# Latent attention: standing values, two heads' products alternating, probabilities scaled by GpSimd before they are turned

## The reference

```python
def chunk_causal_attention(q, k, v):            # q, k: 512 x 16 x 96; v: 512 x 16 x 64
...
        sc = jnp.einsum('bqhd,bkhd->bhqk', qi, k, preferred_element_type=jnp.float32) * scale
        mask = key_chunk[None, :] <= q_chunk[:, None]
        p = jax.nn.softmax(jnp.where(mask, sc, -jnp.inf), axis=-1)
        return jnp.einsum('bhqk,bkhd->bqhd', p.astype(v.dtype), v)

def mla_mixer(h, w_dq, q_norm, w_uq, w_dkv, kv_norm, w_ukv, q_gain, k_gain, w_o):
...
    q = (cq @ w_uq).reshape(b, s, MLA_HEADS, MLA_QK)
...
    kv = (ckv @ w_ukv).reshape(b, s, MLA_HEADS, MLA_NOPE + MLA_V)
    k = jnp.concatenate([kv[..., :MLA_NOPE], k_rope], axis=-1)
    v = kv[..., MLA_NOPE:]
    q = rms_norm_2(q, q_gain)
    k = rms_norm_2(k, k_gain)
...
    o = chunk_causal_attention(q, k, v)
    return o.reshape(b, s, MLA_HEADS * MLA_V) @ w_o
```

## Time and profile before

| | us |
|---|---|
| median of 3 runs | 1928.76 (1928.29 to 1929.55) |
| the profiled execution | 1928.52 |
| its span in the profile | 1926.7 |
| TensorE busy over the span | 1912.5 (99%) |
| VectorE | 1215.8 (63%) |
| ScalarE | 940.2 (49%) |
| GpSimd | 49.9 (3%) |
| share of TensorE in the chain that ended last | 96% |
| granted TensorE clock | 0.9 or more in all 40 slices |

### The profile page before, as it was taken

One profiled execution on the slowest core, in us unless ns is written; L12 is line 12 of the kernel. 1 busy time (PEld: TensorE's weight loads), 2 busy tenths in 40 slices (PEclk: granted clock), 3 DMA queues, 4 the chain that ended last, 5 costly groups with the idle time before them and its releaser, 6 DMA issues.

```text
span 1926.7 us, 23396 instructions
## 1 busy us (share of the span) xinstructions
PE 1912.5 (99%) x9546; PEld 1624.5 (84%) x9546; DVE 1215.8 (63%) x1653; ACT 940.2 (49%) x1332; POOL 49.9 (3%) x85
## 2 busy tenths in 40 slices
PE   8999999999999999999999999999999999999999
PEld 6889998888888888898888888888888889888887
DVE  5645553345767676876745868667644357776867
ACT  5333334234645445568754644545565546453543
POOL 1000000000000000010000000000000000000000
PEclk9999999999999999999999999999999999999999
DMA  7233322322341431321013142241232223414141
GB/s 250 76 98 96 92 68 97 110 99 88 108 136 41 153 110 65 103 59 46 23 45 127 49 153 83 92 153 44 89 110 66 88 66 110 142 55 153 36 140 69
DMA packets 163398, 182.47 MB, mean 95 GB/s; under 512 B 7682, under 2 KB 125015, under 8 KB 163163
## 3 DMA queue, kind: packets, MB, share of 16 engines
q1 hardware_dynamic: 160746, 176.67, 28.6%
q0 software_dynamic: 2528, 4.29, 0.8%
q10 hardware_dynamic: 16, 0.00, 0.0%
HBM read 175.62 MB, written 2.11 MB: 92 GB/s over the span
## 4 chain that ended last, share of the span: by engine, by line
PE 96%; DVE 2%; ACT 1%; DMA 0%; issue 0%; SPq 0%; ACTq 0%
PE psum L96 29%; PE psum L98 29%; PE psum L97 29%; PE psum L2274 2%; PE psum L2252 2%; PE psum L2706 1%; PE psum L2262 1%; DVE weights_lo L414 1%; PE psum L578 1%; PE psum L2230 1%; PE psum L2694 0%; PE psum L1025 0%; PE psum L1017 0%; PE psum L996 0%; PE psum L1006 0%; PE psum L994 0%
## 5 line engine op out<-in xcount | busy, mean ns | idle before, releaser
L96 PE MATMUL psum<-norm_T_hi,weights_hi 128*128 128x512 f32 (+1 forms) x1440 | 538.2, 374 | 0.2 <-DVE weights_lo L414 0.2
L98 PE MATMUL psum<-norm_T_hi,weights_lo 128*128 128x512 f32 (+1 forms) x1440 | 533.7, 371 | 0.0
L97 PE MATMUL psum<-norm_T_lo,weights_hi 128*128 128x512 f32 (+1 forms) x1440 | 533.3, 370 | 0.0
L414 DVE TENSOR_TENSOR weights_lo<-raw_weights,weights_hi 128x2048 fp32r<-128x2048 f32 (+3 forms) x136 | 299.1, 2199 | 240.6 <-ACT weights_hi L408 240.4
L408 ACT ACTIVATE weights_hi<-raw_weights 128x2048 fp32r<-128x2048 f32 (+3 forms) x136 | 249.4, 1834 | 189.3 <-PE psum L98 189.3
L98 PEld LDWEIGHTS psum<-norm_T_hi,weights_lo 128*128 128x128 f32 x1440 | 271.2, 188 | 46.8
L96 PEld LDWEIGHTS psum<-norm_T_hi,weights_hi 128*128 128x128 f32 x1440 | 271.3, 188 | 45.9 <-DVE weights_lo L414 0.5
L97 PEld LDWEIGHTS psum<-norm_T_lo,weights_hi 128*128 128x128 f32 x1440 | 271.4, 188 | 45.2
L96 PE MATMUL psum<-weights_hi,act_T_hi 128*128 128x512 f32 (+1 forms) x528 | 204.0, 386 | 0.0
L98 PE MATMUL psum<-weights_hi,act_T_lo 128*128 128x512 f32 (+1 forms) x528 | 203.0, 384 | 0.0
L97 PE MATMUL psum<-weights_lo,act_T_hi 128*128 128x512 f32 (+1 forms) x528 | 202.9, 384 | 0.0
(11 more groups left out here) (317 smaller groups left out, 2458.2 us busy)
## 6 DMA issues: line engine op xcount, KB each, us to landing
raw_weights<-in_ffn_w_dram SPq DMA_DIRECT2D x32, 1024.0 KB, 5.6
scratch<-in_ffn_w_dram SPq DMA_DIRECT2D x32, 1024.0 KB, 5.4
raw_weights<-in_w_in_dram SPq DMA_DIRECT2D x26, 512.0 KB, 5.3
raw_weights<-in_w_in_dram SPq DMA_DIRECT2D x11, 1024.0 KB, 5.3
raw_weights<-in_w_up_dram SPq DMA_DIRECT2D x8, 1024.0 KB, 6.9
scratch<-in_w_up_dram SPq DMA_DIRECT2D x8, 1024.0 KB, 6.8
raw_weights<-in_w_down_dram SPq DMA_DIRECT2D x8, 1024.0 KB, 5.4
scratch<-in_w_down_dram SPq DMA_DIRECT2D x8, 1024.0 KB, 5.2
```

Source lines behind the costliest of these rows:

```text
L96: pe.matmul(out, ah, bh, start=start, stop=False, skip_group_check=more)
L97: pe.matmul(out, ah, bl, start=False, stop=False, skip_group_check=more)
L98: return pe.matmul(out, al, bh, start=False, stop=stop, skip_group_check=more)
L414: dve.tensor_tensor(WL[:, u % 2, 0:c], raw(units[u].slot)[:, 0:c], WH[:, u % 2, 0:c].bitcast(F32), SUB).then_inc(w_lo, 1)
```

## The change

**Products.** `values` now takes a pair of heads. The values of one key tile j stand (128 x 64), and the turned probabilities of all query tiles that need it stream through: 384, 384, 256 and 128 columns, and 128 for the block (0, 0), which has a place of its own. The results come out already turned, head 2p in partitions 0 to 63 and head 2p + 1 in 64 to 127 of bank 6; the instructions of the two heads alternate. The transposes of a pair, the column of ones and the division are gone; `pair_hi` (ScalarE) and `out_lo` (VectorE) read bank 6.

**Scaling.** The exponentials give their running sums (`accum_out`). VectorE inverts them (`factors`: one reciprocal for t = 3 after the first exponential, one for the rest after the last), GpSimd multiplies the probabilities in `SB` by them, four instructions a head, and only then are they turned: `turn` waits for the scaling (`psc`) in place of the exponential (`pex`).

**Places.** `PT` has two buffers of 2048 columns, one per head of a pair; the turned queries and the products of the rotation move to room behind the activations. The products of a pair stand behind the first two projection tiles at heads 1, 3, 5 and 7, and behind the scores, ahead of the transposes, at heads 10, 12 and 14; the last pair is in the tail. The key-value projections of groups 2 and 3 wait for the products that still read the values which they overwrite.

```diff
-                for t in ORDER:
-                    if t == 2:
-                        pe.wait_ge(a1.sem, a1.at(n + 1))
-                    elif t != 0:
-                        pe.wait_ge(pte.sem, pte.at(2 * n + (1 if t == 3 else 2)))
-                    for j in range(t + 1):
-                        mm = pe.matmul(PS[:, 6, t * MV1:t * MV1 + MV1], PT[:, off[t] + j * P:off[t] + j * P + P],
-                                       VN[:, n // 4 % 2, j, n % 4, :], start=j == 0, stop=j == t)
+                def values(pair):
+                    n = 2 * pair + 1
+                    pe.wait_ge(pte.sem, pte.at(2 * n + 2))
+                    pe.wait_ge(a1.sem, a1.at(n + 1))
+                    if pair:
+                        pe.wait_ge(paired.sem, paired.at(pair))
+                        pe.wait_ge(tl.sem, tl.at(pair))
+                    for j in range(NT):
+                        t = max(j, 1)
+                        for b in range(2):
+                            h = n - 1 + b
+                            pe.matmul(PS[b * MV:b * MV + MV, OUT, t * P:S], VN[:, h // 4 % 2, j, h % 4, :], PT[b][:, j, t:NT, :],
+                                      start=j == 0, stop=True, skip_group_check=j > 0)
+                    for b in range(2):
+                        h = n - 1 + b
+                        mm = pe.matmul(PS[b * MV:b * MV + MV, OUT, 0:P], VN[:, h // 4 % 2, 0, h % 4, :], PT[b][:, 3, 2, :],
+                                       start=True, stop=True)
...
                     scores(n + 1)
+                    if n > MH // 2 and n % 2 == 0:
+                        values(n // 2 - 1)
                     turn(n, 0)
...
-                    for what in before:
+                    for what in gemms[:2]:
                         job(what)
-                    values(n)
-                    for what in gemms:
+                    if n < MH // 2 and n % 2:
+                        values(n // 2)
+                    for what in gemms[2:]:
                         job(what)
...
                         act.wait_ge(gemm, gb + 8 * g + 4 + t + 1)
+                        if g > 1:
+                            act.wait_ge(pvd.sem, pvd.at(2 * g - 2))
...
+                for n in range(MH):
+                    for c in range(2):
+                        pool.wait_ge(rcp.sem, rcp.at(2 * n + c + 1))
+                        for t in (ORDER[:1], ORDER[1:])[c]:
+                            z = SB[:, off[t]:off[t] + (t + 1) * P]
+                            pool.tensor_scalar(z, z, rden[:, n % 2, t:t + 1], None, MUL).then_inc(psc.sem, 1)
+                    if n in (4, 8):
...
+                def factors(n):
+                    for c, ts in enumerate((slice(3, 4), slice(0, 3))):
+                        dve.wait_ge(pex.sem, pex.at(4 * n + (1, 4)[c]))
+                        if n > 1:
+                            dve.wait_ge(psc.sem, psc.at(4 * n - 4))
+                        dve.reciprocal(rden[:, n % 2, ts], den[:, n % 2, ts]).then_inc(rcp.sem, 1)
```

126 lines of the change are left out of this document (55 added, 71 removed).

## The result

| | median of the runs, us | lowest to highest | span of the profiled execution | granted clock over the span |
|---|---|---|---|---|
| before | 1928.8 | 1928.3 to 1929.6 | 1926.7 | 1.00 |
| after | 1955.2 | 1947.1 to 1956.3 | 1953.8 | 0.99 |

The ratio is 1.013, its 95% interval 1.0119 to 1.014: the change costs 26 us, 1.3%. The forecast was 1933.2 us with a range to 1949; the time lies above the range. The direction was right and the size was not. The head loop's first scores start at 867.19 us after and at 866.59 before, so nearly all of it comes later than that.

The account below looks back on a forecast made before the run. TensorE, busy 145.1 of 147.0 us at full clock, was taken to bound the stretch. Terms: -18.1 + 9.6 + 8.1 + 2.3 + 1.9 + 1.9 - 1.1 = +4.7 us on 1928.5, so 1933.2 us, range 1929 to 1949.

Parts of the forecast that it names:

- 18.1 us less on TensorE: Head loop: value products and pair transposes of 38.4 us go, new products at 2.54 us a pair cost 20.3.
- the serial rival: TensorE doesn't overlap the two heads' products: 4.42 us a pair, 15.0 us more, 1948 us; chance 0.20.
- 1.2 us behind the key copy, at eight heads: TensorE idle before the next scores at heads 0, 4 and 8 to 13, waiting for ScalarE's key copy: 9.6 us.
- Heads 0, 4, 7 and 12: Stretches from one head's scores to the next: +1.3, -1.4, +1.3 and +1.1 us against before.
- Last head, 1.9 us: Next stage's output product waits for the masks, with 2.6 us of products and pair transposes no longer ahead: 1.9 us.
- Running sums, 4 x 0.1 us: ScalarE's four exponentials of a head each take 0.1 us more for writing a running sum.
- GpSimd's price: GpSimd's scaling costs 0.2 us + 1.2 ns a column: 0.8 us for 512 columns, 1.5 us for the first three.
- The clock: TensorE's clock stays at 1.00; below 1.00 in the stage was a sign of being wrong, making every term larger.
- VectorE beside GpSimd: Two-input VectorE work slows GpSimd; with the table load at head 10 counted 0.6 us, more clashes one or two.
- dear GpSimd: Rival: GpSimd scales at the two-input price, 8 to 10 us more, 1942 us; chance 0.12.
- Cheap: Rival: GpSimd scales at the price of filling, about 3 us less, 1930 us; chance 0.13.
- faster: Rival: the longer way through ScalarE, VectorE and GpSimd is never late, 1923 us; chance 0.07.

Follow-up runs that it names:

- product form: Changed kernel with GpSimd's scaling written as a product of two tensors, the reciprocal repeated along the columns: 1946.5 us.
- product form, filled, small VectorE work: Changed kernel with scaling as two-tensor product, TensorE's gaps filled with identity transposes, VectorE's key normalisation and rotation cut to a sliver: 1935.4 us.
- product form, filled: Changed kernel with GpSimd's scaling as a product of two tensors and TensorE's gaps filled with unread transposes of the identity: 1939.1 us.

## Why the prediction was wrong

The 26.4 us come apart so, each from one pair of kernels, in this order:

| step | from, us | to, us | share |
|---|---|---|---|
| clock at full level (gaps filled) | 1955.2 | 1944.4 | 10.8 |
| GpSimd near the forecast's price (product form) | 1944.4 | 1939.1 | 5.3 |
| VectorE not beside GpSimd | 1939.1 | 1935.4 | 3.7 |
| the rest, over the kernel before | 1935.4 | 1929.0 | 6.4 |

The last line is taken against 1929.0 us, the kernel before as measured beside that run, so the shares sum to 26.2. The forecast's +4.7 us belongs beside the last line. The terms are tied: at the full price the gaps are longer and the clock falls more. In the other order the price comes first with 8.7 us (1955.2 to 1946.5) and the clock second with 7.4 (to 1939.1), so neither can be called the larger; together they are 16.1 us.

**Step by step.** With the three missed terms out, the times from one head's scores to the next can be laid beside the forecast's terms. The table has the change against before of such stretches, from the starts of the scores in the timelines (for instance head 4: 918.90 - 913.57 = 5.33 us after, 913.88 - 907.14 = 6.74 before, -1.41). The forecast is its sum for that head: values and pair transposes gone, products new, its idle terms.

| stretch of head | forecast | product form, filled, small VectorE work | product form, filled | after |
|---|---|---|---|---|
| 0 | +1.3 | +1.2 | +1.2 | +2.9 |
| 1 | +1.3 | +1.8 | +2.6 | +3.3 |
| 3 | +1.3 | +2.1 | +2.1 | +2.1 |
| 4 | -1.4 | -1.4 | -1.4 | -1.4 |
| 5 | +2.2 | +2.0 | +2.7 | +5.6 |
| 7 | +1.3 | +1.2 | +1.2 | +1.2 |
| 9 | +0.8 | +0.8 | +1.6 | +3.8 |
| 10 | +1.7 | +0.7 | +2.0 | +3.6 |
| 11 | +1.1 | +1.2 | +1.5 | +3.8 |
| 12 | +1.1 | +1.1 | +1.1 | +3.9 |

Heads 2, 6 and 8 are left out: -2.6, -2.6 and -1.4 in the forecast and in every kernel. Head 13 has -0.1 in the forecast, and +0.1, +0.1 and +0.7. Over the loop the forecast has 2.9 us, with the old waits of 1.1 us taken off, and the kernel with small VectorE work 4.3. In the profile of that kernel 1.0 us more lies ahead of the first scores (867.63 us for 866.59), where nothing was changed; this start lies between 866.2 and 867.6 us in the profiles.

- *The working*: its terms sum to 4.6 and not 4.7 us. Filling has 0.67 ns a column by its two rows, not 0.69. Its cases give 0.25 for "within" and 0.68 for "slower", for 0.27 and 0.66. Nothing hangs on these.
- *18.1 us less on TensorE*: right, and 1.8 us better. A pair took 2.31 us for the forecast's 2.54, and the serial rival is dead: it takes the other order of instructions to make it true (4.08 us a pair, 12 us). Nor did the change between the whole array and its halves cost much: the first product of a pair starts 889.85 - 889.58 = 0.27 us behind the last projection product, where these follow each other at 0.17.
- *1.2 us behind the key copy, at eight heads*: right in place and number, 1.04 us each, 8.3 in all for 9.6.
- *Heads 0, 4, 7 and 12*: right within 0.2 us. Head 3 was 0.8 low.
- *Last head, 1.9 us*: right within 0.5 us. From the last scores to the end of the last value products before takes 1005.76 + 2.34 - 986.66 = 21.4 us. The product form with fills is 1.7 us longer there, and the forecast 2.2: 2 x 2.54 for the last two pairs, less 2 x 2.18 and 0.44 (the other pair's transposes stood behind this stretch, at 1012.13), and the 1.9. The changed kernel is 3.9 longer, with the clock at 0.95 from 1020 us on.
- *Running sums, 4 x 0.1 us*: right. At 918.74 the four exponentials of head 5 start, and the last sum is out at 921.20 + 0.19 = 921.39: 2.65 us for the 2.28 of the earlier trace rows.
- ***GpSimd's price* failed.** "One input and one output lie between; I take 0.2 + 1.2 ns a column." The form with a factor for each partition takes 1.56 us for 512 columns and 0.92 for 256, so about 0.28 us + 2.5 ns a column, twice the value taken and above the two-input product that was the upper end (1.27 us). An instruction with fewer inputs was taken as cheaper on an engine of which the trace had no such row. The Trainium skill (GPSIMD Engine Reference, Engine selection) calls one-input operations there roughly line-rate. The rows go against it for this form.
- ***The clock* failed.** The forecast kept it at 1.00 and only named a lower one as what would make it wrong. Its own terms had 1 to 2 us of idle time in a row at heads that have little work, and with the true price they became 3.1 and 1.0 us close together. The scores then took 4.4 us in place of 2.2. Part of that lies on the path: against the kernel with fills the stretch of head 1, whose scores took 2.2 us more, is only 0.4 us longer (+3.33 for +2.97), that of head 12 is 2.8 us longer (+3.93 for +1.10). Taken first it is 10.8 us, taken behind the price 7.4. The Trainium skill (TensorE: Matmul & The Clock Gate, HAM oscillation) describes waits, for DMA in its case, that throttle the clock for the work behind them. The trace agrees, here with waits for GpSimd and ScalarE: the scores at 879.25 took 4.43 us for 2.21. This was the rule to weigh against the change.
- ***VectorE beside GpSimd* was undersized.** The forecast saw the clash and counted 0.6 us for it with the table load. It met the scalings for 3.7 us, even at the lower price: 0.7 to 0.8 us each at heads 1, 5 and 9, where the ring is late, 1.2 at head 10, where it is the key scaling, and 0.3 at head 11. The prediction's reading that the two engines block each other whole fits GpSimd's product form nearly (1.6 us lost beside 1.75) and the form with a factor less (0.92), and VectorE's 1536-wide product was not held up at all.
- The other rivals: *dear GpSimd* (1942 us) was the right mechanism at too small a price, and the time of the changed kernel at the full clock, 1944.4, lies near it. *Cheap* and *faster* are out: even with scaling left out the time is 1930.3.

The forecast's way of counting gives a few microseconds less than the 1930.2 measured with no scaling. Part of this shows in the traces. The last head is 3.7 us longer there than before and not 1.7: 1.6 of the difference is the half clock behind the gap of 1.95 us, shown above. And the copies, which the forecast put at nothing, are late: TensorE waits 4.5 us in seven waits for ScalarE's copy of the turned probabilities (L2404), where it waited 1.1 us in four before. What it would be worth to have that copy earlier stays open; no run changed it alone.

## What to carry to other kernels

Work taken off a busy engine can be worth nothing once the loop behind it is a ring through other engines: here 18 us less on TensorE, even with the added step left out, gave no gain. When a change opens gaps on TensorE, price them twice, once as idle time and once as work behind them at half the clock, and test the second by filling the gaps with work that nobody reads. For an instruction form that the trace doesn't have on that engine, take no bound from forms with fewer or more inputs; and before moving work to an idle engine, look what the busy one costs (0.49 us on VectorE for 1.56 on GpSimd).

## What the runs showed of the hardware

- On GpSimd the multiplication by a factor for each partition took 1.56 us for 128x512 f32 as an operation with one tensor, and 1.04 us written as a product with the factor repeated along the columns. A product of two full tensors took 1.27 us. The same operation took 0.49 us on VectorE.
- TensorE's granted clock went to the 1.2 GHz level behind gaps of 2.0 to 3.1 us with shorter ones of 0.6 to 1.0 us close by, and behind one of 3.2 us where the gap of 1.0 was filled. Over 866 to 1040 us it was 0.88, with the short gaps filled 0.95, with the long ones 0.99, with both 1.00. The fills were transposes of the identity.
- Products in the two column halves of the array overlapped when they alternated between the halves (2.31 us for 20 instructions) and hardly when the same 20 came half by half (4.08 us).
- GpSimd was held up by VectorE passes from SBUF to SBUF with one input as well as with two. The form with a factor lost 0.63 and 0.53 us for each microsecond of them, the product form 0.91 beside the pass with two.
- The start of the next exponential on ScalarE came about 0.1 us later where each wrote a running sum (2.65 us for four, 2.28 without).
